# Two feed-forward layers with the gate and up weights held stationary, and a first weight unit loaded in single pieces

## The reference

```python
D_MODEL = 1024; SEQ = 256; DEPTH = 2; D_FF = 2816

def rms_norm(x, g):
    x32 = x.astype(jnp.float32)
    y = x32 * lax.rsqrt(jnp.mean(x32 * x32, axis=-1, keepdims=True) + RMS_EPS)
    return (y * g.astype(jnp.float32)).astype(x.dtype)

def swiglu(u, w_gate, w_up, w_down):
    return (jax.nn.silu(u @ w_gate) * (u @ w_up)) @ w_down

# first_block
for layer in range(DEPTH):
    u = rms_norm(h, g_mix[layer])
    h = h + (mla_stick_breaking_mixer if layer % 2 == 0 else chunk_band_mixer)(u, ...)
    u = rms_norm(h, g_ffn[layer])
    h = h + swiglu(u, w_gate[layer], w_up[layer], w_down[layer])
# second_block: projections, three kinds of attention, gates, output product
```

## Time and profile before

| | |
|---|---|
| time of the profiled execution | 978.15 us |
| its span on the core | 976.4 us |
| TensorE busy | 968.8 us (99%) |
| TensorE weight loads (overlap the matmuls) | 796.5 us (82%) |
| VectorE busy | 623.1 us (64%) |
| ScalarE busy | 593.0 us (61%) |
| DMA | 169.37 MB, mean 173 GB/s |
| matmuls of gate and up (bank `pair_ps`, lines 519 to 521) | 960, of 395, 390 and 389 ns mean |
| matmuls of down (line 577) | 528, of 389 to 390 ns mean |

### The profile page before, as it was taken

One profiled execution on the slowest core, in us unless ns is written; L12 is line 12 of the kernel. 1 busy time (PEld: TensorE's weight loads), 2 busy tenths in 40 slices (PEclk: granted clock), 3 DMA queues, 4 the chain that ended last, 5 costly groups with the idle time before them and its releaser, 6 DMA issues.

```text
span 976.4 us, 13095 instructions
## 1 busy us (share of the span) xinstructions
PE 968.8 (99%) x4936; PEld 796.5 (82%) x4936; DVE 623.1 (64%) x765; ACT 593.0 (61%) x918; POOL 17.1 (2%) x30
## 2 busy tenths in 40 slices
PE   9999999999999999999999999999999999999998
PEld 7888788888888877788888888887878888788887
DVE  5776775555556767565555555867676667786654
ACT  6777665454445665464545445876767768857571
POOL 1000000000000000000000000000000000000000
PEclk9999999999999999999999999999999999999999
DMA  8536256756554553447666655565544443346551
GB/s 279 186 117 209 86 198 195 254 172 214 173 195 144 179 172 130 130 156 254 219 210 193 224 184 172 106 239 174 166 136 136 147 148 135 130 141 207 207 178 44
DMA packets 106078, 169.37 MB, mean 173 GB/s; under 512 B 4196, under 2 KB 65590, under 8 KB 106032
## 3 DMA queue, kind: packets, MB, share of 16 engines
q1 hardware_dynamic: 103392, 161.23, 50.5%
q0 software_dynamic: 2304, 7.40, 2.4%
q10 hardware_dynamic: 336, 0.10, 0.0%
HBM read 167.56 MB, written 1.16 MB: 173 GB/s over the span
## 4 chain that ended last, share of the span: by engine, by line
PE 97%; DVE 1%; DMA 1%; ACT 0%; issue 0%; SPq 0%; ACTq 0%
PE acc L519 14%; PE acc L521 14%; PE acc L520 14%; PE acc L577 12%; PE pair_ps L521 7%; PE pair_ps L519 7%; PE pair_ps L520 7%; PE acc L934 3%; PE acc L636 3%; PE turn_ps L725 2%; PE acc L754 1%; PE turn_ps L595 1%; PE pair_ps L708 1%; PE pair_ps L704 1%; PE turn_ps L519 1%; PE turn_ps L521 1%
## 5 line engine op out<-in xcount | busy, mean ns | idle before, releaser
L1992 DVE TENSOR_TENSOR w_lo<-w_raw,w_hi 128x2048 fp32r<-128x2048 f32 (+3 forms) x154 | 342.9, 2230 | 129.9 <-ACT w_hi L1252 129.6
L1252 ACT ACTIVATE w_hi<-w_raw 128x2048 fp32r<-128x2048 f32 (+3 forms) x154 | 286.4, 1863 | 87.4 <-PE acc L521 35.3
L519 PE MATMUL acc<-w_hi,uT_hi 128*128 128x512 f32 (+3 forms) x456 | 179.7, 394 | 2.3 <-DVE w_lo L1992 1.2
L521 PE MATMUL acc<-w_hi,uT_lo 128*128 128x512 f32 (+3 forms) x456 | 174.1, 382 | 0.0
L520 PE MATMUL acc<-w_lo,uT_hi 128*128 128x512 f32 (+3 forms) x456 | 173.8, 381 | 0.0
L519 PE MATMUL pair_ps<-w_hi,uT_hi 128*128 128x512 f32 x320 | 126.5, 395 | 0.0
L521 PE MATMUL pair_ps<-w_hi,uT_lo 128*128 128x512 f32 x320 | 124.9, 390 | 0.0
L520 PE MATMUL pair_ps<-w_lo,uT_hi 128*128 128x512 f32 x320 | 124.6, 389 | 0.0
L519 PEld LDWEIGHTS acc<-w_hi,uT_hi 128*128 128x128 f32 x456 | 85.7, 188 | 21.8 <-issue 4.2
L521 PEld LDWEIGHTS acc<-w_hi,uT_lo 128*128 128x128 f32 x456 | 85.6, 188 | 16.8
L520 PEld LDWEIGHTS acc<-w_lo,uT_hi 128*128 128x128 f32 x456 | 85.9, 188 | 14.3
(11 more groups left out here) (273 smaller groups left out, 1335.6 us busy)
## 6 DMA issues: line engine op xcount, KB each, us to landing
w_raw<-in_w_in SPq DMA_DIRECT2D x46, 1024.0 KB
w_raw<-in_w_gate SPq DMA_DIRECT2D x44, 512.0 KB
w_raw<-in_w_up SPq DMA_DIRECT2D x44, 512.0 KB
w_raw<-in_w_down SPq DMA_DIRECT2D x22, 1024.0 KB
w_raw<-in_w_out SPq DMA_DIRECT2D x12, 1024.0 KB
w_raw<-in_w_qkv SPq DMA_DIRECT2D x16, 512.0 KB
w_raw<-in_w_branch SPq DMA_DIRECT2D x6, 1024.0 KB
w_raw<-in_w_qkv SPq DMA_DIRECT2D x4, 1024.0 KB
```

What stands on the lines that cost most here:

```text
L519: mm(o, xh, wh[:, k, :], start=first and k == 0, stop=False)
L521: done = mm(o, xl, wh[:, k, :], start=False, stop=last and k == len(kts) - 1)
L1252: activation(w_hi[:, slot, 0:width], w_raw[:, slot, 0:width], ACT.Copy).then_inc(hi_done, 1)
L1992: v.tensor_tensor(w_lo[:, slot, 0:width], w_raw[:, slot, 0:width], w_hi[:, slot, 0:width].bitcast(f32), ALU.subtract).then_inc(lo_done, 1)
```

## The change

In both feed-forward parts:

- The input's parts lie side by side in one tile `uT` (tile, part, 256 tokens). In `step_unit` the *weights* are stationary. For each of four groups of 128 columns (two of gate, two of up) and each of four input tiles, one matmul with the high weights runs over 512 columns (high input beside low input) and one with the low weights over the 256 high ones. The results are turned already: hidden columns on the partitions, tokens along the free dimension. Each group has a PSUM bank: `pair_ps` for gate, `turn_ps` for up, in all steps. The first half of a bank has two of the products, the second half the third, so they must be added.
- The four transposes per step (`turn_hidden`) and `last_step` go.
- ScalarE copies the second halves to SBUF (gate at `gate_done`, up at `unit_used`), VectorE adds the first halves, and multiplies the gate by a row of scales.
- The scale of the norm now varies along the free dimension. VectorE makes a diagonal of the scales once a layer, TensorE spreads it with one product by ones (256 columns), ScalarE copies it to SBUF. The up side's scale is applied when `acc` is added to `h` (`add_quarter` with a factor).
- TensorE's `step_unit` waits for `gate_read` of the step before ahead of its first group and for `up_read` ahead of its third.

At the start: the first unit comes in four single tiles, the second in halves; the input tiles go in five groups of 1, 1, 2, 2 and 2; `keep_busy` after the transposes is 5 instead of 8.

```diff
-        uT_hi = sb("uT_hi", [P, KT, S], f32r)
-        uT_lo = sb("uT_lo", [P, KT, S], f32r)
+        uT = sb("uT", [P, KT, 2, S], f32r)
...
+        uT_hi, uT_lo = uT[:, :, 0, :], uT[:, :, 1, :]
+        flat_hid = flat_qkv[:, 1024:1536]
+        up_lo = flat_qkv[:, 1536:2048].rearrange("p (b c) -> p b c", b=TB)
+        diagonal = flat_qkv[:, 0:S]
+        scale_now = square_flat[:, 0:S]
...
+        input_banks = [(acc[2][:, :], 0, 1), (pair_banks[0], 1, 1), (pair_banks[1], 2, 2), (turn_banks[0], 4, 2),
+                       (turn_banks[1], 6, 2)]
...
+            unit_in_parts(0, [(k, 1, (row_full + raw_full)[k]) for k in range(4)])
+            unit_in_parts(4, [(0, 2, second_full), (2, 2, raw_full[1])])
...
# TensorE
-            def swiglu(norm):
+            def swiglu(layer, norm):
+                step_banks = pair_banks + turn_banks
                 def step_unit(c, k0):
                     pe.wait_ge(lo_done, n.unit + 1)
+                    wh, wl = unit_parts(4, 2 * FT)
+                    for b in range(4):
+                        if k0 == 0 and b == 0:
+                            since(pe, gate_read, t0 + c)
+                        if k0 == 0 and b == 2:
+                            since(pe, up_read, t0 + c)
+                            if n.late is not None:
+                                late, n.late = n.late, None
+                                late()
+                        for k in range(4):
+                            kt = k0 + k
+                            if n.fresh is not None and b == 0 and kt in n.fresh:
+                                pe.wait_ge(turned_lo, n.fresh[kt])
+                            w = [part[:, k, P * b:P * b + P] for part in (wh, wl)]
+                            mm(step_banks[b], w[0], uT[:, kt, :, :].rearrange("p i t -> p (i t)"), start=kt == 0, stop=False)
+                            done = mm(step_banks[b][:, 0:S], w[1], uT[:, kt, 0, :], start=False, stop=kt == KT - 1)
+                        if k0 and b == 1:
+                            done.then_inc(gate_done, 1)
...
+                def down(c, first):
+                    pe.wait_ge(hid_lo, t0 + c + 1)
+                    proj_unit((0, 1), first, False)
                 def step(c, first):
                     step_unit(c, 0)
-                    turn_hidden(c - 1)
                     step_unit(c, 4)
-                    down(c - 1, first, False)
+                    down(c - 1, first)
...
                 step_unit(0, 0)
                 step_unit(0, 4)
+                pe.wait_ge(diag_ready, layer + 1)
+                mm(acc[3][:, 0:S], ones[:, 0:P], diagonal, start=True, stop=True).then_inc(scale_spread, 1)
                 step(1, True)
+                with pe.Fori(2, NF) as c: ...
+                pe.wait_ge(hid_lo, t0 + NF)
                 closing_unit(2, norm=norm)
# ScalarE; its swiglu is: slot_step, slot_step, the copy of scale_now, gate(0), step(1), ...
+                act.wait_ge(scale_spread, layer + 1)
+                activation(scale_now, acc[3][:, 0:S], ACT.Copy).then_inc(scale_row, 1)
                 def gate(c):
+                    act.wait_ge(gate_done, t0 + c + 1)
+                    activation(hid_e, pair_ps[:, :, S:2 * S], ACT.Copy).then_inc(gate_copied, 1)
+                    act.wait_ge(gate_scaled, t0 + c + 1)
+                    link(activation(hid_e, hid_g, ACT.Exp, scale=-1.0))
                     link(activation(hid_e, hid_e, ACT.Ln, bias=1.0))
                     activation(hid_e, hid_e, ACT.Exp, scale=-1.0).then_inc(gate_exp, 1)
+                    act.wait_ge(unit_used, n.unit)
+                    activation(up_lo, turn_ps[:, :, S:2 * S], ACT.Copy).then_inc(up_copied, 1)
                 def step(c): # slot_step, split_hidden(c - 1), slot_step, gate(c), slot_step, as before
# VectorE
                 def gate(c):
+                    dve.wait_ge(gate_copied, t0 + c + 1)
+                    v.tensor_tensor(hid_g, pair_ps[:, :, 0:S], hid_e, ALU.add).then_inc(gate_read, 1)
...
+                    v.tensor_tensor(hid_g, hid_g, scale_now.unsqueeze(1).broadcast_to([P, TB, S]), ALU.mult)\
+                        .then_inc(gate_scaled, 1)
+                    dve.wait_ge(up_copied, t0 + c + 1)
+                    v.tensor_tensor(hid, turn_ps[:, :, 0:S], up_lo, ALU.add).then_inc(up_read, 1)
                     dve.wait_ge(gate_exp, e0 + c + 1)
+                    link(v.tensor_tensor(hid_g, hid_g, hid_e, ALU.mult))
+                    v.tensor_tensor(hid, hid, hid_g, ALU.mult).then_inc(u_ready, 1)
```

More of the change, by code:

```diff
@@ L260, in build_program @@
         gate_exp = sem("gate_exp")
+        gate_done = sem("gate_done")
+        gate_copied = sem("gate_copied")
+        up_copied = sem("up_copied")
+        gate_read = sem("gate_read")
+        gate_scaled = sem("gate_scaled")
+        up_read = sem("up_read")
+        diag_ready = sem("diag_ready")
+        scale_spread = sem("scale_spread")
+        scale_row = sem("scale_row")
+        hid_hi = sem("hid_hi")
+        hid_lo = sem("hid_lo")
         tab_done = sem("tab_done")
@@ L541, in chunk_unit, with unit_in_parts @@
                     n.chunk = n.chunk + 1
-            def unit_in_halves(kt0, between=None):
-                count = kt0 // 4 + 1
-                for k0, ready in ((0, first_lo), (2, lo_done)):
+            def unit_in_parts(kt0, split, between=None):
+                for k0, m, ready, count in split:
                     if between and k0:
@@ L661, in closing_unit @@
                 n.late = late
-                n.fresh = n.bank
+                n.fresh = {2 * i: n.bank + i + 1 for i in range(4)}
                 n.bank = n.bank + 4
@@ L1105, in first_mixer @@
                 closing_unit(2, 3, FFN0)
-            def swiglu(norm):
-                n0, b0 = n.written, n.bank
+            def swiglu(layer, norm):
+                t0 = NF * layer
+                step_banks = pair_banks + turn_banks
                 def step_unit(c, k0):
                     pe.wait_ge(lo_done, n.unit + 1)
[L1113 to L1119, removed]
+                    wh, wl = unit_parts(4, 2 * FT)
[10 more added lines that the diff above has]
+                            if n.fresh is not None and b == 0 and kt in n.fresh:
+                                pe.wait_ge(turned_lo, n.fresh[kt])
+                            w = [part[:, k, P * b:P * b + P] for part in (wh, wl)]
[3 more added lines that the diff above has]
+                            done.then_inc(gate_done, 1)
+                    if k0:
+                        n.fresh = None
@@ L1164, in swiglu @@
[L1164 to L1166 removed]
+                n.unit = u0 + 3 * (NF - 2)
+                n.written += NF
+                pe.wait_ge(hid_lo, t0 + NF)
                 closing_unit(2, norm=norm)
```

202 lines of the change are left out of this document (93 added, 109 removed).

## The result

The changed kernel takes 987.13 us (986.79 to 987.4, four executions) beside 980.25 for the kernel before (979.02 to 981.82): a ratio of 1.0071, 95% interval 1.0054 to 1.0087, +6.9 us. The forecast was 983.1, +2.8, range 979.5 to 987.5. Sign and range hold; four of the seven microseconds were not in the sum, and the measured time lies near the upper end of the range. The profiled execution has a span of 985.5 us and a time of 987.30.

The account below looks back on a forecast made before the run. TensorE was taken as the bound, busy 968.8 of 976.4 us at full clock. Two layers at +1.95 give +3.9, the start -1.0, total +2.9, carried over to the median of 980.27: 983.1 us, range 979.5 to 987.5.

Parts of the forecast that it names:

- Units, +2.35 a layer: Gate/up units on TensorE: 32 matmuls instead of 24, same columns, +0.107 us each, 22 units a layer; bounds 0 and 2.35.
- the rival with it hidden: Gate/up units: the fixed part of short matmuls is hidden behind long ones, total 978.4 us; chance 0.04.
- its sign of being wrong: New gate/up units: the prediction is wrong if a distance of 256 columns is not 0.120 us.
- Transposes, -5.17: Feed-forward loop: 11 sets of transposes of `hid` a layer go, at 0.47 us each, saving 5.17 us.
- Waits of step 1, +3.6: Between step 0 and step 1: spreading product 0.45, TensorE waits of 1.9 and 1.05 us plus restarts, +3.6 us a layer.
- First group and last step, +1.15: Layer's first group waits for its third input tile, +0.6 us; closing unit waits for the last hidden tile, net +0.55.
- Sum of a layer: Each feed-forward layer: 2.35 - 5.17 + 3.6 + 0.6 + 0.55 = +1.95 us, two layers +3.9.
- main case: Whole kernel: the forecast of 983.1 us itself, with a range of its own of 981.3 to 985.2; chance 0.74.
- Start, -1.0: Kernel start: first real matmul 1.6 us earlier, third unit then waits 0.45 + 0.11; 1.0 us kept, bounds 0 and 1.6.
- Clock rival: Step 1's two waits bring TensorE back to 1.2 GHz, losing 1.9 us in each layer, total 986.9; chance 0.10.
- no waits: Step 1's waits aren't there since reads come earlier than program order suggests, total 976.8 us; chance 0.05.
- a start that gives nothing: Kernel start: small transfers land at 8.15 us or later, so nothing is gained, total 984.1 us; chance 0.07.

Follow-up runs that it names:

- handover shortened: Changed kernel with spreading product inside step 0's second unit, VectorE's additions ahead of its second subtraction and ScalarE's up copy ahead of its exponentials: 979.34 us, ratio 1.0010.
- twos: Changed kernel with two matmuls of 512 columns, then two of 256, in turn: 984.51 us in one execution, steps of 16.59 us.
- ones: The changed kernel's own order, matmuls of 512 and 256 columns alternating one by one: 987.13 us, steps of 16.79 or 16.80 us.
- fours: Changed kernel with each group's four matmuls of 512 columns first, then its four of 256: 984.72 us, ratio 1.0061.
- sixteens: Changed kernel with, in steps 2 to 10, all 16 matmuls of 512 columns of a unit first, then all 16 of 256: 984.7 us, ratio 1.0059.
- A product put in on purpose: Changed kernel with one unused float32 product of 128 columns added per loop step, ahead of the first unit's third group: steps of 16.98 us in one execution.

## Why the prediction was right in sign and short by four microseconds

- **Units, +2.35 a layer: mis-sized.** This is the step that failed: "A unit costs 24 x 0.2267 = 5.44 before and 16 x (0.2267 + 0.1200) = 5.55 after, +0.107." The fixed part was real (no trace has it hidden, and the rival with it hidden is out), but it was taken for the upper bound. The forecast looked at one side of the mixture only, "that a 256 behind a 512 costs what a 256 behind a 256 does", and that side was safe: 0.117. The side that it didn't look at, a 512 behind a 256, costs 0.236 where it took 0.2267. So its sign of being wrong, a 256 that is not 0.120, would hardly have found the error. The alternating stream costs 0.353 a pair, 0.0066 more than the two rows give; over the 352 pairs of the first layer less the 24 fast ones that is 2.2 us, and the down unit after it 0.06 more, in ten units 0.6: +2.8. Why the bound was wrong can be seen in the kernel before: it had 512s behind 512s and 256s behind 256s, and no row of the mixture. The nearest rows were the 512s behind the transposes of `hid`, mostly at 0.23 to 0.236 for the next six or eleven matmuls; the forecast booked them to the transposes' 0.47.
- **Transposes, -5.17: held.** A step without them is 16.57 in the best order, which is 16.79 - 0.47 + 2 x 0.107 = 16.53 and 0.04 for the mixture.
- **Waits of step 1, +3.6: held** (3.56; with the handover shortened 6.4 us were won in two layers). The reason was half the story: VectorE's two subtractions were as late as ScalarE's copy.
- **First group and last step, +1.15: +0.75.** Waits of 0.35 and 0.49 for 0.5 and 0.75.
- **Sum of a layer:** 1.95 + 2.8 - 0.4 = 4.35, measured 4.2 and 4.4.
- **The range held by luck.** The main case had a range of its own of 981.3 to 985.2, and 987.13 is outside it; it is also just above the sum's own upper bound (+6.8, where +6.9 was measured). It lies inside 979.5 to 987.5 where the clock's case was put (986.9), and the clock was full in all four executions.
- **Start, -1.0: held within 0.4 to 1.4**, by another wait than the one named: ScalarE's scaling behind two roundings.
- **Clock rival, 0.10:** not in the result's executions, but real in one trace, by the mean clock in 5 of 27 executions, and cheap where it was traced (0.5 us or less and not 1.9), since it eats the second wait. Its 1.9 came from the pace of the dummy products at the start. The row of granted clock doesn't show that stretch as slow: a window from 1.15 to 5.00 us says 1.00, as does one from 7.55 to 9.50. That the lower clock nearly doubles the distance is shown in the trace with twos (0.85 us where 0.47 is the pace).
- The other rivals (no waits, a start that gives nothing, a hidden fixed part) are out.

## What to carry to other kernels

Price a stream of instructions by a row of that very stream: distances of 512s among 512s and 256s among 256s did not add up to the distance of the two in turn, and the order alone moved a step by 0.2 us. When all steps share the same banks, the first step is the one with no other work between its end and its successor, so put its emptying ahead of bulk work in the program of each engine. When a chain is shortened by moving bulk work behind it, look at what stands behind the bulk work.

## What the runs showed of the hardware

- 32 matmuls of 512 and 32 of 256 columns, a step less its down unit: (16.79 - 5.50) / 32 = 0.353 us a pair in ones, (16.59 - 5.45) / 32 = 0.348 in twos, (16.69 - 5.49) / 32 = 0.350 in fours, (16.57 - 5.47) / 32 = 0.347 in sixteens. The cost doesn't follow the number of turns. In ones a 512 takes 0.236 and a 256 takes 0.117; among their like they take 0.2267 and 0.120. In ones there are two steady paces, 0.353 in all steps from the second on, and either 0.347 or 0.353 behind each wait of step 1, not always the same in two layers or two executions; behind the spreading product inside step 0 (shortened handover) it was 0.347 in both layers. A product put in on purpose did not bring the faster one. The cause is open.
- Behind a wait of 1.84 us TensorE's granted clock was at 1.2 GHz for some 3.4 us in both layers of one trace, and at 2.4 GHz behind a wait of 1.8 us in seven other traces. It cost 0.3 to 0.5 us each time, since the next wait took the rest.
